# Attention in a decoder step: GpSimd divides the probabilities before the turn, instead of VectorE dividing the values after it

## The reference

```python
def sparse_core(q, k_sel, v_sel, valid):
    s = jnp.einsum("bthd,btkhd->bthk", q, k_sel, preferred_element_type=jnp.float32) * (DH_ATT ** -0.5)
    s = jnp.where(valid[:, :, None, :], s, -jnp.inf)
    p = jax.nn.softmax(s, axis=-1).astype(v_sel.dtype)
    o = jnp.einsum("bthk,btkhd->bthd", p, v_sel)

def mem_attend(qm, mk, mv):
    s = jnp.einsum("bthd,bmhd->bthm", qm, mk, preferred_element_type=jnp.float32) * (DH_MEM ** -0.5)
    p = jax.nn.softmax(s, axis=-1).astype(mv.dtype)
    o = jnp.einsum("bthm,bmhd->bthd", p, mv)
```

## Time and profile before

| | before |
|---|---|
| median of 3 runs | 2951.62 us (2948.67 to 2954.58) |
| profiled execution | 2958.25 us |
| its span | 2956.7 us, mean granted clock 0.983 |
| busy PE, PEld | 2820.5 us (95%), 2677.3 us (91%) |
| busy DVE, ACT, POOL | 2312.6 (78%), 1215.4 (41%), 1140.6 us (39%) |
| busy share of POOL in the attention stage | 0 |

### The profile page before, as it was taken

The page is one execution under the profiler, slowest core; times in us unless marked ns, Lnnn a source line. Parts: engine busy times, 40 slices in busy tenths (PEclk is TensorE's granted clock), DMA queues, the critical chain, the costliest instruction groups (busy, mean ns, idle before and its releaser), DMA issues. The chain is left out here.

```text
span 2956.7 us, 56695 instructions
## 1 busy us (share of the span) xinstructions
PE 2820.5 (95%) x21274; PEld 2677.3 (91%) x21274; DVE 2312.6 (78%) x3773; ACT 1215.4 (41%) x2361; POOL 1140.6 (39%) x808
## 2 busy tenths in 40 slices
PE   6999989999999999999988899899989999899999
PEld 6999989999989999999986666599889999899999
DVE  8888897777748999999994566647388888977776
ACT  5444444434433333324444555512244444434443
POOL 4555544555443332223331000021355555444552
PEclk8999999999999999999998999999999999999999
DMA  5332323332232222222227888734433333233331
GB/s 161 92 95 88 106 73 94 94 93 87 71 100 84 78 87 78 86 72 59 81 81 253 296 270 267 242 112 155 135 98 100 94 95 107 74 98 101 93 99 56
DMA packets 359405, 340.33 MB, mean 115 GB/s; under 512 B 16831, under 2 KB 293666, under 8 KB 359134
## 3 DMA queue, kind: packets, MB, share of 16 engines
q1 hardware_dynamic: 354430, 330.41, 36.2%
q0 software_dynamic: 4128, 4.20, 0.5%
q10 hardware_dynamic: 576, 2.10, 0.2%
HBM read 299.60 MB, written 37.05 MB: 114 GB/s over the span
## 5 line engine op out<-in xcount | busy, mean ns | idle before, releaser
L294 PE MATMUL bank<-op_r_ffn,w_hi 128*128 128x256 f32 (+1 forms) x2992 | 583.8, 293 | 33.1 <-DVE op_r_ffn L275 17.2
L294 PEld LDWEIGHTS bank<-op_r_ffn,w_hi 128*128 128x128 f32 x2992 | 478.5, 192 | 40.0 <-issue 35.8
L294 PE MATMUL bank<-op_r_ffn,w_lo 128*128 128x256 f32 (+1 forms) x1496 | 435.6, 291 | 0.0
L294 PE MATMUL bank<-h_hi,w_hi 128*128 128x362 f32 (+1 forms) x1272 | 423.6, 333 | 6.2 <-ACT qi L2024 2.6
L435 POOL TENSOR_TENSOR w_lo<-sums_ffn,w_hi 128x512 fp32r<-128x512 f32 x214 | 317.5, 1493 | 266.4 <-ACT w_hi L431 266.4
L294 PE MATMUL bank<-h_lo,w_hi 128*128 128x362 f32 (+1 forms) x1272 | 419.5, 330 | 0.0
L294 PE MATMUL bank<-h_hi,w_lo 128*128 128x362 f32 (+1 forms) x1272 | 419.0, 329 | 0.0
L294 PE MATMUL bank<-op_r_ffn,more_hi_ffn 128*128 128x288 f32 (+1 forms) x1936 | 375.0, 292 | 14.2 <-ACT s_ffn L575 5.4
L294 PEld LDWEIGHTS bank<-op_r_ffn,more_hi_ffn 128*128 128x128 f32 x1936 | 306.6, 190 | 18.1 <-issue 8.6
L435 POOL TENSOR_TENSOR more_lo_ffn<-sums_ffn,more_hi_ffn 128x512 fp32r<-128x512 f32 x138 | 205.5, 1496 | 227.8 <-ACT more_hi_ffn L431 227.8
L294 PEld LDWEIGHTS bank<-op_r_ffn,w_lo 128*128 128x128 f32 x1496 | 288.3, 193 | 0.0
(11 more groups left out here) (434 smaller groups left out, 6985.0 us busy)
## 6 DMA issues: line engine op xcount, KB each, us to landing
raw<-in_w_ffn_in SPq DMA_DIRECT2D x132, 512.0 KB, 3.9
raw_ffn<-in_w_ffn_out SPq DMA_DIRECT2D x88, 512.0 KB, 3.5
v_ring<-in_cache_v SPq DMA_DIRECT2D x128, 256.0 KB, 4.6
raw<-in_w_in SPq DMA_DIRECT2D x53, 512.0 KB, 5.1
raw_ffn<-in_w_ffn_in SPq DMA_DIRECT2D x44, 512.0 KB, 3.8
kt_two<-in_cache_k SPq DMA_DIRECT2D x88, 256.0 KB, 3.6
kept_g<-stage SPq DMA_DIRECT2D x24, 544.0 KB, 3.1
gate<-kept_g SPq DMA_DIRECT2D x24, 544.0 KB, 3.7
```

The source lines that it names most:

```text
L294: mm = pe.matmul(out, left, right, start=(start and i == 0 and j == 0), stop=(stop and i == n - 1 and j == 2))
```

## The change

GpSimd multiplies the probabilities by their inverse sums in place, between the exponential and the turn. The tiles `inv` and `inv_t`, the spreading of the sums, their transposes and the copies out of PSUM go. DVE's product after the values becomes a plain copy. Inverses are no longer counted among the turns, so that the numbers of all later turns shift, and with them the engine and the bank of each.

```diff
@@ attention_plan
-        if entry[0] in ("turn", "inverse", "pt", "mpt", "ot", "mot"):
+        if entry[0] in ("turn", "pt", "mpt", "ot", "mot"):
...
-        if 0 <= d - 2 < n:
-            add(d, "inverse", d - 2)
         sample(d, 0)
...
                 add(d, "turn", d - 1, g, min(4, blocks - g))
-            add(d, "invert", d - 1)
         if d < n:
             add(d, "exp", d)
+            add(d, "invert", d)
@@ attention, new
+    def on_pool(pool):
+        for d in range(n):
+            pool.wait_ge(inverted, d + 1)
+            for e in range(2):
+                c, p_ = col(d, e), probabilities(d, e)
+                pool.tensor_scalar(p_, p_, rinv[:, c:c + 1], None, ALU.mult).then_inc(divided, 1)
@@ on_pe, turn
-                pe.wait_ge(exped, 2 * d + (1 if g + w <= blocks_of(d) // 2 else 2))
+                pe.wait_ge(divided, 2 * d + (1 if g + w <= blocks_of(d) // 2 else 2))
@@ on_pe, inverse
-                pe.wait_ge(spread, d + 1)
-                for e in range(1 if doubles[d][0] == "att" else 2):
-                    mm = pe.transpose(tb[:, e * P:(e + 1) * P], inv[:, e, :], ident[:, :])
@@ on_dve, invert
                 dve.wait_ge(exped, 2 * d + 2)
-                if d >= 1:
-                    dve.wait_ge(turned, turn_of[("inverse", d - 1)] + 1)
+                if d >= 4:
+                    dve.wait_ge(divided, 2 * d - 6)
                 dve.reciprocal(rinv[:, c:c + 2], rsum[:, c:c + 2]).then_inc(inverted, 1)
-                dve.wait_ge(inverted, d + 1)
-                if doubles[d][0] == "att":
-                    dve.tensor_copy(inv[:, 0, :].rearrange("p (e n) -> p e n", e=2),
-                                    rinv[:, c:c + 2].unsqueeze(2).to_broadcast([P, 2, DH])).then_inc(spread, 1)
-                else:
-                    dve.tensor_copy(inv[:, :, :], rinv[:, c:c + 2].unsqueeze(2).to_broadcast([P, 2, P])).then_inc(spread, 1)
@@ on_dve, values
-                wait_turn(dve, turn_of[("inverse", d)])
-                dve.tensor_tensor(to, bank[6][:, 0:w], inv_t[:, :, :].rearrange("p e n -> p (e n)")[:, 0:w], ALU.mult).then_inc(normed, 1)
+                dve.tensor_copy(to, bank[6][:, 0:w]).then_inc(normed, 1)
```

More of the change, by code:

```diff
@@ L926, in decoder_step @@
                 nc, sem, mem, bank, feed2, x, raw, w_hi, w_lo, qT, qmT, x_kept, I, scratch)
-            (att_sp, att_pe, att_act, att_dve, att_prefetch, att_first_values, att_clear, att_queries, att_keys, att_lows,
+            (att_sp, att_pool, att_pe, att_act, att_dve, att_prefetch, att_first_values, att_clear, att_queries, att_keys, att_lows,
              att_blocks) = attention(
@@ L957, in _ @@
                     kh_pool(pool, att_clear)
+                    att_pool(pool)
                     mg_pool(pool)
@@ L2886, in attention @@
     ptm = place("ptm", [P, 2, P], F32, 6144)
-    inv = place("inv", [P, 2, P], F32, 7168)
-    inv_t = place("inv_t", [P, 2, P], F32, 73248)
     q_hi = place("q_high", [P, SEQ], F32R, 8192)
@@ L2937, in attention @@
     scored, topped, maxed = sem("scored"), sem("topped"), sem("maxed")
-    exped, inverted, spread = sem("exped"), sem("inverted"), sem("inverse_spread")
+    exped, inverted, divided = sem("exped"), sem("inverted"), sem("divided")
     mk_gained = sem("mk_gained")
@@ L3007, in evict @@
             copy(pt[:, g:g + w, :], b[:, 0:w * P].rearrange("p (g n) -> p g n", n=P)).then_inc(evicted[me], 1)
-        elif kind == "inverse":
-            d = entry[1]
-            w = 1 if doubles[d][0] == "att" else 2
-            if d >= 1:
-                eng.wait_ge(normed, d)
-            copy(inv_t[:, 0:w, :], b[:, 0:w * P].rearrange("p (e n) -> p e n", e=w)).then_inc(evicted[me], 1)
         elif kind == "pt":
@@ L3216, in on_pe @@
                 mm.then_inc(valued, 1)
-            elif kind == "inverse":
-                d = s
-                pe.wait_ge(spread, d + 1)
-                for e in range(1 if doubles[d][0] == "att" else 2):
-                    mm = pe.transpose(tb[:, e * P:(e + 1) * P], inv[:, e, :], ident[:, :])
-                mm.then_inc(turned, 1)
             elif kind == "sc":
@@ L3473, in attention @@
         turned=(turned, n_turns), act_evicted=(evicted[0], (n_turns + 1) // 2), dve_evicted=(evicted[1], n_turns // 2)))
-    return on_sp, on_pe, on_act, on_dve, prefetch, first_values, clear_blocks, first_queries, first_keys, first_lows, sample_blocks
+    return on_sp, on_pool, on_pe, on_act, on_dve, prefetch, first_values, clear_blocks, first_queries, first_keys, first_lows, sample_blocks
 EARLY_PRODUCTS = 2
```

## The result

| | before | after |
|---|---|---|
| median of 4 runs each | 2953.1 us (2948.67 to 2954.94) | 3024.87 us (3021.82 to 3027.53) |
| ratio, 95% interval | | 1.0242 [1.0227, 1.0257] |
| profiled execution, its span | 2958.25, 2956.7 us | 3021.82, 3020.2 us |
| mean granted clock | 0.983 | 0.973 |

What follows compares the result with a forecast made beforehand. TensorE was taken as close to the bound, in a ring with ScalarE and VectorE that GpSimd would join. Terms 6.0 + 0.3 - 0.8 + 2.4 gave +7.9 us: 2959.5 us against the 2951.62 median, range 2948 to 2978.

Steps and rivals of the forecast that it cites:

- The price on GpSimd: Multiplying 1024 columns: 1.04 us, from the select's 285 ns plus 0.835 ns a column; bounds 952 and 2446 ns.
- the sum: Three rounds 6.0, first round 0.3, end of stage -0.8, clock 2.4: +7.9 us in all.
- Rival (c): GpSimd multiplies at its rate for two tensors, 2.40 us for 1024 columns: +38, 2990 us; chance 0.12.
- double 15: The sample group's turn comes first and GpSimd's two times 0.93 us fit beside it: no further delay.
- double 13: Attention round's 1024-wide double: TensorE waits for GpSimd's two multiplications, its turns finishing 1.7 us late.
- Double 17: The round's 768-wide double: its turns wait for GpSimd; delay 1.2 us before it, 2.7 after.
- Double 19: The round's 640-wide double: its turns wait for GpSimd; delay 2.45 us before it, 2.85 after.
- Double 23: A 256-wide memory double late in the round: input there at 1771.5, TensorE at 1771.2; round +2.0 us.
- The clock: One drop of TensorE's granted clock in every round instead of two of four: 2 x 1.2 = 2.4 us.
- The gain: 64 small transposes leave TensorE's order: 13.9 us, the whole gain if nothing replaces them, and nothing hides it.
- VectorE at its reciprocal: VectorE, held until ScalarE is done, isn't missed: its next maximum needs scores TensorE makes after the turn.
- a sign of a wrong mechanism: TensorE not waiting for GpSimd before turn 13, or VectorE's maxima starting late because of the reciprocal.

Runs made afterwards that it cites:

- filler: Changed kernel, with TensorE transposing the identity, read by nobody, ahead of the turns of the doubles 1024, 768 and 640 wide: 3006.2 us, ratio 1.0169.
- short_divide: Changed kernel, with GpSimd multiplying only the first 16 columns of each half: 2958.94 us, ratio 1.0013 to the kernel before.
- no_divide: Changed kernel without GpSimd's multiplications, the turns waiting for the exponentials alone and values left undivided: 2953.89 us, ratio 0.9993 to the kernel before.

## Why the prediction was wrong

- **The price on GpSimd** is the step that failed ("I take it with the slope of the fill"). 1.04 us was taken, 2.84 measured. Neither end of my bounds held: the operation with two tensors, 2.40 to 2.45 us, was meant as the upper end, and the real one is above it. The half of the rule that the sum followed, roughly line rate with one input (the Trainium skill, GPSIMD Engine Reference, Engine selection), isn't what these runs show: 2842 ns against VectorE's 0.75 us for 1024 columns is 3.8 times, and with a constant it is still 2768 ns. The factor of two that the Trainium skill gives at the same place for two inputs doesn't meet it either. VectorE's work beside it can hardly be the reason: in the slice 1720 to 1724 above GpSimd is busy for 3.93 us and VectorE for only 0.69. No run had VectorE quite still. The prediction named a row of 1.5 us or more as its sign of a wrong size. Rival (c) was nearest, with 2990 us at 0.12.
- **The mechanism of the waits held, with double 15 overlooked.** Put the measured prices into the same steps: double 13 is 5.3 late (GpSimd's start at 1706.2, two times 2.84, 0.15 and 0.87, against 1707.61). Double 15, for which the prediction had "no further delay", adds 1.7: TensorE waits 1.36 us for GpSimd at the doubles of its width in the first and third round (at 1649.46 and 1834.37), and in the other two the sample's turn ahead of it takes 3.4 us instead of 1.94. Double 17: 6.5 before it, 1732.46 + 6.5 + 0.455 + 2 x 2.20 + 0.15 + 0.87 = 1744.8, so 10.8 late. Double 19: 13.3. Double 23: 13.8. filler's second round, at a clock of 0.96, bears this out: its turns of 13, 15, 17 and 19 end 5.4, 7.1, 11.1 and 13.4 us later than before, counted from the round's first widest exponential, and the round ran from 1713.19 to 1799.75, 86.56 us: 13.8 more than the 72.72 before. In the changed kernel that round was 20.9 longer; the difference of 7.1 goes with its clock of 0.85. The waits are at the places named, and narrow even doubles had none.
- **The clock** was the second term that was mis-sized: it was given 2.4 us. The changed kernel and short_divide issue the same matmuls in the stage (3225 and 3224 in the windows rows), and TensorE is busy for 286.30 against 256.33 us with them: 30 us more, at 0.88 instead of 0.98. In the same two rows TensorE is idle for 79.2 against 42.8 us, 36.4 more. Filling the waits gave 20 us back. I priced a drop by one round that had one; here almost each long wait has one behind it.
- **The gain** was wrong too: "this is the whole gain ... nothing hides it". no_divide shows that the 13.9 us weren't to be had, or only a small part of them. The transposes stood in TensorE's order, but behind them the values needed a copy of VectorE's that wasn't done, and the sample's turn an exponential of ScalarE's. The prediction said of the idle time there that it mostly isn't gained; it holds of the transposes beside it too. The sum hid this error, since it was small beside the first. Even with GpSimd at 1.04 us the sum of +7.9 would probably have been too low: VectorE's multiplication of 0.75 us already cost 9 us. A straight line between 0.33 us (+4) and 1.57 us (+32) gives an estimate of 4 + 28 x 0.71 / 1.24 = +20 for 1.04 us. At 0.75 us the same line gives +13, where VectorE's run had +9, so +20 is probably too high.
- **VectorE at its reciprocal.** The prediction's reason, that the next maximum needs scores made after the turn, doesn't hold for double 14: its scores stand ahead of turn 13. Its maxima do start late, which was named as a sign of a wrong mechanism: at 1718.16, right behind the reciprocal that waited 2.44 us for ScalarE, so 2.55 us after double 13's first exponential started (1715.61), where before it was 1.61 (1703.76 to 1705.37). It cost nothing there, since VectorE then waits 3.13 us for the turn itself.

```profile
1705.37 0.48 DVE L3406 CUSTOM_DVE_ANT_0 pb_even<-bank,bias,rq 128x256 f32<-128x256 f32 x1 [1.14 <-PE bank L3185]
```

- **Right**: the direction, and the path of the delay with its hand-overs. VectorE's rows beside a busy GpSimd are no longer than before, e.g. 0.48 us for the maximum of 256 columns in both rows shown, so GpSimd didn't slow VectorE here.

The 71 us, then: some 4 for hand-overs, order and the shortest passes (short_divide), 20 to 30 for the clock, and the rest, around 40, waiting for GpSimd itself. The last two can't be divided more sharply, since the fillers don't fit the waits exactly: TensorE still waits 11.0 us for GpSimd in filler.

## What to carry to other kernels

An idle engine is no free engine when it is put into a chain that the bound engine waits on: its time per element, measured for that very operation, decides, and rows of other operations don't bound it. Ask of work that you remove from the bound engine what would have been waited for in its place; an experiment that removes it and adds nothing answers that before any replacement is built. A wait that the profile puts down to an engine is checked against what the program waits for. Price waits of TensorE together with the clock that they lose behind them.

## What was not expected of the hardware

- GpSimd's multiplication of float32 by a scalar takes 2.5 ns a column from 128 to 1024 columns, whether the scalar is a constant (530 and 2768 ns) or one for each partition (602 and 2842 ns). With 16 columns it takes 0.33 us.
- That is slower than its operation on two tensors (2442 ns for 1024 columns in the page's groups of the same execution).
- Useless transposes made a kernel 20 us faster, since they kept TensorE's granted clock at 0.97 instead of 0.88.
